# A two-model fp32 transformer kernel on one core: products of the input blocks grouped by size, and the work around three normalisations, the differential attention and the retention reordered

## The reference, cut to what matters

```python
def _swiglu(xn, w_in, w_out):
    a, b = jnp.split(xn @ w_in, 2, axis=-1)
    return (jax.nn.silu(a) * b) @ w_out
...
for i in range(DEPTH):
    h = x + 0.5 * _swiglu(_rms(x, ffn1_norm[i]), ffn1_w_in[i], ffn1_w_out[i])
    xn = _rms(h, mix_norm[i])
    m = _diff_attention(xn, ...) if kind == 0 else _retention(xn, ...)
    h = h + m.astype(h.dtype)
    x = h + 0.5 * _swiglu(_rms(h, ffn2_norm[i]), ffn2_w_in[i], ffn2_w_out[i])
```

## Time and profile before

| | |
|---|---|
| Time, median of 3 runs | 1460.09 us (1459.99 to 1462.83) |
| Profiled execution: its own time | 1459.89 us |
| Profiled execution: span of its instructions | 1458.1 us |
| Busy: PE, PEld | 98%, 82% |
| Busy: DVE, ACT, POOL | 62%, 50%, 9% |
| Granted TensorE clock, mean | 0.998 of full speed |
| Read from memory | 251.20 MB |

### The profile page before, as it was taken

The page is one execution under the profiler, slowest core; times in us unless marked ns, Lnnn a source line. Parts: engine busy times, 40 slices in busy tenths (PEclk is TensorE's granted clock), DMA queues, the critical chain, the costliest instruction groups (busy, mean ns, idle before and its releaser), DMA issues.

```text
span 1458.1 us, 21483 instructions
## 1 busy us (share of the span) xinstructions
PE 1429.0 (98%) x7983; PEld 1202.3 (82%) x7983; DVE 902.3 (62%) x1057; ACT 721.9 (50%) x921; POOL 125.7 (9%) x110
## 2 busy tenths in 40 slices
PE   8999999999999999999999999999999989999999
PEld 7888887778888888888888778888887778888887
DVE  5665666757566676666644445666665775576564
ACT  5445455555545454444544444554445754354442
POOL 0000012451000010000000110000001142010000
PEclk9999999999999999999999999999999999999999
DMA  8655655325656556566654534655666312155552
GB/s 260 214 187 182 225 188 188 130 84 177 196 180 196 191 173 193 184 199 194 226 187 146 177 140 159 207 197 174 197 210 211 128 59 89 59 183 192 187 189 86
DMA packets 157771, 253.10 MB, mean 174 GB/s; under 512 B 9824, under 2 KB 101648, under 8 KB 157456
## 3 DMA queue, kind: packets, MB, share of 16 engines
q1 hardware_dynamic: 154736, 247.21, 51.7%
q10 hardware_dynamic: 2976, 5.07, 1.0%
HBM read 251.20 MB, written 1.05 MB: 173 GB/s over the span
## 4 chain that ended last, share of the span: by engine, by line
PE 91%; DVE 4%; ACT 3%; issue 2%; DMA 1%; POOL 0%; SPq 0%; ACTq 0%; DVEq 0%; POOLq 0%
PE bank L1862 14%; PE bank L1864 14%; PE bank L1863 14%; PE bank L1936 13%; PE bank L1933 13%; PE bank L1935 7%; PE bank L1934 7%; ACT w_hi L580 1%; DVE w_lo L1258 1%; PE bank L1874 1%; PE bank L2310 1%; DMA x<-in_x 1%; PE bank L2234 0%; DVE kT L1628 0%; PE bank L2343 0%
## 5 line engine op out<-in xcount | busy, mean ns | idle before, releaser
L1258 DVE TENSOR_TENSOR w_lo<-raw,w_hi 128x2048 fp32r<-128x2048 f32 x226 | 518.0, 2294 | 351.2 <-ACT w_hi L580 350.7
L580 ACT ACTIVATE w_hi<-raw 128x2048 fp32r<-128x2048 f32 x229 | 437.0, 1910 | 228.8 <-PE bank L1934 144.4
L1936 PE MATMUL bank<-xT,w_hi 128*128 128x512 f32 x832 | 295.4, 397 | 0.0
L1933 PE MATMUL bank<-xT,w_hi 128*128 128x512 f32 (+1 forms) x848 | 294.4, 393 | 0.0
L1934 PE MATMUL bank<-xT,w_lo 128*128 128x256 f32 (+1 forms) x848 | 234.2, 276 | 0.0
L1935 PE MATMUL bank<-xT,w_lo 128*128 128x256 f32 x832 | 233.7, 281 | 0.0
L1862 PE MATMUL bank<-w_hi,xT 128*128 128x512 f32 x524 | 211.0, 403 | 2.4 <-DVE w_lo L1258 1.7
L1864 PE MATMUL bank<-w_hi,xT 128*128 128x512 f32 x524 | 204.7, 391 | 0.0
L1863 PE MATMUL bank<-w_lo,xT 128*128 128x512 f32 x524 | 204.2, 390 | 0.0
L1864 PE MATMUL bank<-w_hi,hT_lo 128*128 128x512 f32 x484 | 188.7, 390 | 0.0
L1933 PEld LDWEIGHTS bank<-xT,w_hi 128*128 128x128 f32 x848 | 159.3, 188 | 35.4 <-DVE xT L1354 0.3
(11 more groups left out here) (318 smaller groups left out, 1205.8 us busy)
## 6 DMA issues: line engine op xcount, KB each, us to landing
raw<-in_ffn_w_in SPq DMA_DIRECT2D x174, 512.0 KB, 4.7
raw<-in_ffn_w_out SPq DMA_DIRECT2D x88, 512.0 KB, 4.2
raw<-in_w_ff SPq DMA_DIRECT2D x64, 512.0 KB, 4.2
raw<-in_rt_w_in SPq DMA_DIRECT2D x48, 512.0 KB, 4.6
raw<-in_w_in SPq DMA_DIRECT2D x28, 512.0 KB, 4.8
raw<-in_da_w_in SPq DMA_DIRECT2D x24, 512.0 KB, 4.7
raw<-in_rt_w_out SPq DMA_DIRECT2D x16, 512.0 KB, 4.1
raw<-in_da_w_out SPq DMA_DIRECT2D x8, 512.0 KB, 4.1
```

The source lines that it names most:

```text
L580: act.activation(w_hi[:, n % RING, :], raw[:, n % RING, :], ACT.Copy).then_inc(hi_ready, 1)
L1258: dve.tensor_tensor(w_lo[:, n % RING, :], raw[:, n % RING, :], w_hi[:, n % RING, :].bitcast(F32), ALU.subtract).then_inc(lo_ready, 1)
L1933: pe.matmul(out, hi[:, k, cols], mov, start=first_of, stop=False)
L1936: return pe.matmul(out, hi[:, k, cols], mov, start=False, stop=k == 3)
```

## The change

Five things change in the code.

1. `whole_block` runs, in each group `b`, the four 512-column matmuls together and the four 256-column matmuls together, instead of alternating. The half-token groups after a norm are treated alike.
2. In `norm(1)`, `norm(4)` and `norm(6)`, ACT's `split(n0 + 2)` stands between the first token half's squares and the last quarter's copy.
3. In the differential attention, DVE runs `sum_squares(0, 1)` ahead of `split(n0 + 6)`, `normalise(1, 1)` ahead of `split(n1 + 1)`, and in the loop over heads `maxima(i)` ahead of `head_normed(i - 2)`. ACT runs `turned_out` at the end of an iteration, before the `split` instead of after it.
4. The off-diagonal half of the bias is copied by POOL to `off_bias` in fp32r (in the place of `relu`, which has no use in this phase), and the bias matmul of `scores` for it is fp32r x fp32r instead of fp32 x fp32.
5. Retention's `turn_y(0)` goes to banks 0 and 1 and stands before the last projection block; the turned result goes to `hT_hi`, `hT_lo` instead of `xT`, so that it can be written while `xT` is still read. `turn_y(1)` no longer waits for head 0.

```diff
-                def pair(b, k, tok=None):
...
+                def products(b, tok=None):
...
+                    def upper(k):
+                        mov = flat(xT[:, 4 * j + k, :, :]) if tok is None else xT[:, 4 * j + k, :, half]
+                        return pe.matmul(out, hi[:, k, cols], mov, start=j == 0 and k == 0 and not tok,
+                                         stop=j == 1 and k == 3)
+
+                    def lower(k):
+                        return pe.matmul(cross, lo[:, k, cols], xT_hi[:, 4 * j + k, half], start=False, stop=False)
+
+                    for part in ((upper, lower) if j == 0 else (lower, upper)):
+                        for k in range(4):
+                            mm = part(k)
+                    return mm
...
                     if q >= 2 and g:
                         squares(q - 2)
+                    if q == 2 and g:
+                        split(n + 2)
...
-                norm(1)
-                split(n0 + 2)
+                norm(1, n0)
                 split(n0 + 3)
...
-                for i in range(4, DA_H + 3):
-                    turned_out(i - 3)
+                turned_out(1)
+                for i in range(4, DA_H + 2):
...
                     if i <= DA_H:
                         out_squares(i - 1)
+                    turned_out(i - 2)
                     if i % 2 == 0:
                         split(n1 + (i - 4) // 2 + 2)
+                split(n1 + 5)
...
+                    if m == 11:
+                        turned_y(0)
                     read_chunk(n0, 6, m, rt_chunk[m], ACT.Silu if m >= 8 else ACT.Copy, rt_pair[m])
...
+                pool.tensor_copy(off_bias[:, :, :], bias[:, :, P:T])
                 pool.tensor_copy(diag_bias, bias[:, :, 0:P]).then_inc(bias_full, 1)
...
                 normalise(0, 0)
+                sum_squares(0, 1)
                 split(n0 + 6)
-                sum_squares(0, 1)
                 split(n0 + 7)
...
                 maxima(3)
+                normalise(1, 1)
                 split(n1 + 1)
-                normalise(1, 1)
...
                     turned_out(i - 3)
+                    if i < DA_H:
+                        maxima(i)
                     if i <= DA_H + 1:
                         head_normed(i - 2)
-                    if i < DA_H:
-                        maxima(i)
...
-                        pe.matmul(S[m][:, P:T], bias[:, i, P:T], ident, start=False, stop=True)\
+                        pe.matmul(S[m][:, P:T], off_bias[:, i, :], ident_r, start=False, stop=True)\
                             .then_inc(scores_ready, 1)
...
+                            if h == 3:
+                                pe.wait_ge(proj_read, 6 + 2 * 17)
+                                turn_y(0)
```

78 lines of the change are left out of this document (37 added, 41 removed).

## The result

The changed kernel takes 1447.8 us (median of 4 runs, 1446.9 to 1448.0) where the kernel before took 1461.1 (4 runs, 1460.0 to 1462.8): ratio 0.9905, 95% interval 0.9893 to 0.9917. It is faster by 0.95%, 13.2 us, about half of the 25.2 that were forecast; 1447.8 lies above the upper end of the range, 1446. The profiled execution took 1446.9 us with a span of 1445.1, against 1459.9 and 1458.1.

The account below looks back on a forecast made before the run. The prediction took PE's own stream as the bound, with FFN blocks limited by matmul spacing. Its terms summed to 25.2 us, taking 1460.1 to 1434.9 us; its own range was 1430 to 1442, the scored one up to 1446.

Parts of the forecast that it names:

- grouping by size: FFN input products: four matmuls of one size together save 35.7 ns in each of 404 groups; taken as 13.5 us.
- third weight blocks: At three norms, ACT's earlier split removes PE's waits of 0.86, 0.63 and 1.12 us; 2.6 us.
- retention's first turn: Retention: transposes done before the last projection block are covered by it, removing PE's 2.5 us idle; gain 2.5 us.
- first and third turn of q, k: Attention: short DVE work moved ahead of splits lets the turns start earlier; gains 1.5 and 1.9 us.
- loop over heads: Attention heads: earlier maxima and `turned_out` shorten PE's waits for `turned_mix` before `values`; 3.0 us.
- bias in fp32r: Attention scores: one pass replaces two in 16 bias matmuls, mostly hidden; 0.2 us, range 0 to 1.9.
- which is 11.9 more than 226.9 + 114.8: FFN blocks: an alternating pair's 353.6 ns exceeds same-size spacings, so three of four grouped pairs take 341.7.
- rival A: FFN input products: order of sizes doesn't matter, leaving 11.7 us of gain, 1448.4 us; chance 0.13.
- the forecast's own sign of being wrong: After the change, 256-column matmuls at 0.12 us or more, or `values` waiting for `head_normed`.
- at most 120 ns per load: FFN 256-column runs: full weight-load cost bounded from bias matmuls; at 120 ns grouping saves 8.1 us.
- Between 0 and 4.6 us is possible: Attention head loop: bounds put on the gain from reordering, taken as 3.0 us.
- rival B: Attention: POOL's splits block its head norms and moved splits come late, losing attention's gains; 1441.5 us, chance 0.08.

Follow-up runs that it names:

- the small kernel: Separate kernel computing nothing of the reference: 64 matmuls in various size orders behind 512-column chains, other engines quiet or busy; alternating pairs 11.293 us, groups of four 11.195.
- the second small kernel: Separate TensorE-only kernel varying what precedes the alternating order, and weight widths: 11.293 us from a 512-column chain, 11.157 from four 128-column matmuls, 11.318 from a pause (one repetition).

## Why the prediction was wrong

What the edits are worth in the changed kernel, against the terms of the sum:

```
term                          forecast   measured   how
grouping by size                13.5       3.0      undone 3.1, alone 2.9 (spans)
third weight blocks              2.6       3.05     undone, three stages
retention's first turn           2.5       2.5      retention 3.29 - 0.76
first and third turn of q, k     3.4       3.5      attention 5.77 - 1.09 - 0.51 - 0.67
loop over heads                  3.0       0.5      both orders undone
bias in fp32r                    0.2       0.7      undone
sum                             25.2      13.25     spans 13.0
```

The first line and the spans hold the scatter of `ffn0`, so they are good to no better than some 0.5 us, and that the sums match so closely is in part luck. The two lines of the turns are what is left of a stage when the measured ones are taken away; they were not undone alone, and the places in the trace (1.6 us at the first turn, 1.72 and 0.15 at the third, 2.38 and 0.16 in retention, all gone) agree with them.

**Grouping.** This step failed, and by its size: "which is 11.9 more than 226.9 + 114.8". Order does matter, as forecast, and against the rule of the Trainium skill that the forecast set beside it (TensorE: Matmul & The Clock Gate, "Back-to-back issue gap"), by which nothing changes. That section gives the rule for an isolated matmul, and says that in a stream with weight loads both set the spacing, so it was a weak witness for rival A. The measured pairs, 347 to 353 ns, are all above its 325.

But neither of the two prices carries over. 226.9 ns holds for a 512-column matmul behind five or more of its kind, and the first four behind a run of 256 take 232.5 on average. In groups of four they are the only ones, except in the first group of a run, which stands behind a chain of 512 and takes just the forecast's 1.379 us in the small kernel; the seven behind it take 1.402 on average. The 0.22 us that the forecast read at the first matmul of an FFN block was of that exception. 114.8 came from the earlier trace rows, whose matmuls load 8 columns of weights; with 128 it is 119.9 from the third on, and 256-column matmuls at 0.12 us or more were the forecast's own sign of being wrong. Over a run of 64 a group of four pairs is 1.399 us and not 1.379, against 1.412 before: 12 ns saved, not 35.7.

The text named the weak point itself, bounded it with "at most 120 ns per load" at 8.1 us of gain, and then chose a value near the other end by an argument (a 512-column matmul starts 0.12 us behind a 256-column one) that says nothing about a run of them. Had it taken 119.9 and left 226.9 as it was, it would still have said 8; the slow 512-column matmuls behind a change of size were in no row that it read. They were in the trace: in the earlier trace rows's kind of chain the first distances behind an FFN block are 236, 228, 233 and 231.

**The loop over heads.** This step failed too, 0.5 in place of 3.0. The chain was followed with each operation at its own length, "Between 0 and 4.6 us is possible". The waits before `values` did fall (4.6 to 3.2, where the forecast had about 2), but the mixing of the next maps, now earlier, falls into POOL's 4.6 us split and waits for its end, 1.8 us twice, and the waits at `turn_mix` grow by 2.6. That is the mechanism that rival B had at the wrong operation: it saw POOL's splits block POOL's head norms, not DVE. The run with the splits on DVE gives 1.56 us back at once. Some 0.9 us of the 3.0 stay unaccounted for: no run has the old order of the loops together with the splits on DVE.

**The others.** The third blocks, the turns of q and k, and retention's turn came as forecast, to 0.5 us together, and each in its place. The rule that an idle entry understates the loss by 0.16 us, because the next start could come 0.23 us after the last, was right in its direction and still low: the three waits, forecast at 0.86, 0.63 and 1.12, measured 1.09, 0.76 and 1.20. A part of the rest is the start behind such a wait, which comes late too: 212.35 to 212.68 us in the run with the third blocks back, 0.33 in place of 0.23.

Rival A, at 1448.4, came nearest in time, but not in kind: it gave grouping nothing and the loop 3.0, and the truth is 3.0 and 0.5, which happen to make nearly the same sum. Without the undone runs the total alone would have spoken for a wrong story.

## What to carry to other kernels

A price for "one matmul behind another of its kind" holds for the width of weights and the place in the run where it was read. Before multiplying it by a thousand, take it from four in a row of just that form, or measure 64 of them; the small kernel's 11.195 us were the real kernel's to the nanosecond. When an edit brings an operation of DVE forward, look at what POOL runs at the new time, and not only at what the operation waits for. And compare stages, not totals: whole times differ by 1 to 3 us between runs, the stages behind the first by hundredths to two tenths.

## What was unexpected of the hardware

- Alternating 512- and 256-column matmuls ran in one of two rhythms, 352.9 or 346.7 ns a pair, to the end of their run of 64 or 80. Four 128-column matmuls ahead give the quick one; a chain of 512, a run of 256, one small matmul or a pause of 2.4 us the slow one. Why is open. So is why the price of a 256-column run goes 115.5, 117.8, 113.5, 116.1, 119.9 ns with weights of 8, 32, 64, 96 and 128 columns.
- In the small kernel, work of ACT, DVE and the DMA beside the matmuls changed no distance between them, to 1 ns.
- A DVE operation on 2 numbers a partition took 2.00 us beside a POOL operation of 4.58, while two of its reductions from PSUM in the same stretch (from 289.74 us) took 0.61 us together, as without POOL. Its RECIPROCAL in the same stretch took 0.18 us and wasn't held up either.
- Pauses of some 2 us on PE are sometimes followed by the clock at 1.2 GHz. In the second small kernel the entry from a pause was run three times. Behind 2.38 us of idle time nothing happened; behind 2.46, twice, a part of the matmuls ran at 427 and 213 ns, the clock in the windows from 194 us on being 0.61 and 0.82 of full speed:

```profile
191.00:194.00 3.00, 0.54 (x3) 0.12 (x2) 2.29 (x1) 0.00 (x0) 0.00 (x0) 1.00 0.00 0
194.00:197.00 3.00, 3.00 (x11) 2.58 (x12) 0.00 (x0) 0.00 (x0) 0.00 (x0) 0.61 0.02 5
197.00:200.00 3.00, 3.00 (x16) 2.58 (x15) 0.00 (x0) 0.00 (x0) 0.00 (x0) 0.82 0.00 0
```

The length alone doesn't decide it. From start to start, the pause at `turn_mix` had no such sequel at 2.13 us in the changed kernel and at 2.15 in the one with the alternating order; in the one with groups of two it had one at 2.15, and the stage is 1.7 us longer there. The 2.66 us at retention's second turn in the kernel before had none. So a pause near 2 us can cost 1.7 us on top of itself; the version with the splits on DVE has none above 1.4 us in that loop.
